# Splitting the modulation projection of a transformer layer kernel: the part needed first by feature, the rest by weight slabs inside the next projection

## The chip, the cores and the metric

The kernel runs on one core of a Trainium2 chip. A core has TensorE (PE, matrix multiplication; its weight loads are shown as PEld), VectorE (DVE), ScalarE (ACT), GpSimd (POOL) and SyncE (SP, which here only issues DMAs), and 16 DMA engines that move data between HBM and the on-chip memory SBUF. The metric is the device time of one execution in microseconds (us); the lower, the better.

## The reference, cut to what matters

One layer works on 1024 prompt rows and 32 sample rows of 1024 features. Both sub-layers take a normalised input that is scaled and shifted by a conditioning vector; prompt and sample have one vector each.

```python
def adaln(c, w_ada, b_ada):
    return jnp.split(jax.nn.silu(c) @ w_ada + b_ada, 6, axis=-1)

def modulate(x, g, shift, scale):
    return rmsnorm(x, g) * (1.0 + scale[:, None, :]) + shift[:, None, :]
...
        p_sh1, p_sc1, p_gt1, p_sh2, p_sc2, p_gt2 = adaln(c_prompt, w_ada[l], b_ada[l])
        mp, new_p = mix_prompt(modulate(yp, g_mix_pre[l], p_sh1, p_sc1), w_in[l], w_out[l], ...)
        yp = yp + p_gt1[:, None, :] * rmsnorm(mp, g_mix_post[l])
        fp = swiglu(modulate(yp, g_ffn_pre[l], p_sh2, p_sc2), w_gate[l], w_up[l], w_down[l])
        yp = yp + p_gt2[:, None, :] * rmsnorm(fp, g_ffn_post[l])
```

`w_ada` is 1024 x 6144 floats (25 MB), and its six groups of 1024 columns are shift, scale and gate of the mixing part and shift, scale and gate of the feed-forward part. Only the first two groups are needed before `mix_prompt` projects its input with `w_in`; everything is float32.

## The kernel before

The kernel is a sequence of blocks. In a block each engine has its own instruction stream, the streams meet at semaphores, and a block ends when every stream has ended. The change touches the first two blocks.

`conditioning` computes all 6144 modulation values for the two conditioning vectors. SP loads `w_ada` in 12 column blocks of 512 (2 MB each) into three buffers in turn, with the input rows `x` (four loads of 1 MB and one of the 32 sample rows) between them, and then three pieces of `w_in`. PE takes each column block as 8 matmuls with the two vectors as a 2-column weight and 512 streamed columns (line 299), DVE adds the bias (line 311). The result is a row per vector. To use shift and scale as a value per partition, POOL writes the rows to HBM and reads them back 4 bytes at a time (lines 263 and 267). Meanwhile ACT squares and sums the rows of `x` (line 283), POOL takes the power -0.5 (line 271) and DVE normalises the nine row tiles of `x` (line 329). DVE also makes two bias strips, 8 partitions (one for each head) of 768 and 384 values.

`natural` starts with two DMAs on SP's queue that write each strip 128 times to HBM (lines 414 and 415: `[[0, P], [1, STRIP_A]]`, 3 MB and 1.5 MB, all read from 8 partitions). PE transposes `x` in 17 units (`turn_pe`, lines 352 and 355), ACT and DVE read the units back with scale and shift applied (`turn_read`). PE then projects nine row tiles with 840 columns of `w_in` (line 457: per tile 8 matmuls of 512 and 8 of 328 columns), ACT and DVE copy each tile out, and PE turns the keys (line 466). SP waits for the last tile, loads three weight pieces for the next block (line 528), stores the results (lines 435 and 438) and waits for the strips. The next block, `transposed`, continues with line 604.

Of the kernel before, what the change touches and what calls it, by code (L numbers as in the profile page):

```python
# [27 lines left out]
ALU = mybir.AluOpType  # L28
# [3 lines left out]
P = 128  # L32
D = 1024
# [102 lines left out]
def build(nc, ins, outs):  # L136
    with ExitStack() as ctx:
# [54 lines left out]


STRIPS = X + 6144


def conditioning(ctx, nc, ins, outs, sem, T, T3, B, view, ident, d_ada, **_):
    w_ada = ins["w_ada"][0].rearrange("(p t) n -> p t n", t=KT)
    c_in, b_in, tab_in = sem("c_in"), sem("b_in"), sem("tab_in")
    x_in = [sem(f"x_in{i}") for i in range(5)]  # L200
    ada_in = [sem(f"ada_in{i}") for i in range(3)]
    wnat_in = ctx.wnat_in = sem("wnat_in")
    silu_done, ada_mm, ada_row = sem("silu_done"), sem("ada_mm"), sem("ada_row")
    ss_zero, ss_done, var_done, rstd_done, xn_done = (sem(n) for n in (
        "ss_zero", "ss_done", "var_done", "rstd_done", "xn_done"))
    ident_done, strip_mm, strip_done = (sem(n) for n in (
        "ident_done", "strip_mm", "strip_done"))
    ada_out, gates_out, mod_in, mod_done = sem("ada_out"), sem("gates_out"), sem("mod_in"), sem("mod_done")
    x_at = [KA + D * t for t in range(NT)]
    tab_a, strip_a, tab_b, hot_b, strip_b = (CA + 7168, STRIPS, CA + 7456, CA + 7472, STRIPS + STRIP_A)  # L210
    junk = HT + 7296

    def x_sem(t):
        return x_in[4 if t == SAMPLE else t // 2]


    order = [0, 1, 2, 3, 6, 7, 8, 9, 4, 5, 10, 11]

    with nc.Block() as block:
        @block.sync  # L220
        def _(sp):
            sp.dma_start(T3(R_C, 2, KT)[:, 0, :], ins["c_prompt"][0].rearrange("(p t) -> p t", t=KT)).then_inc(c_in, 16)
            sp.dma_start(T3(R_C, 2, KT)[:, 1, :], ins["c_sample"][0].rearrange("(p t) -> p t", t=KT)).then_inc(c_in, 16)
            xp = ins["x_prompt"][0].rearrange("(t p) d -> p t d", p=P)
            for c in range(12):
                if c >= 3:
                    sp.wait_ge(ada_mm, c - 2)
                sp.dma_start(T3(QA + 4096 * (c % 3), KT, 512), w_ada[:, :, 512 * order[c]:512 * order[c] + 512]).then_inc(ada_in[c % 3], 16)
                if c == 1:
                    sp.dma_start(T(HT, 6 * D, 2), ins["b_ada"][0].partition_broadcast(2)).then_inc(b_in, 16)  # L230
                if 2 <= c < 6:
                    i = c - 2
                    sp.dma_start(T3(x_at[2 * i], 2, D), xp[:, 2 * i:2 * i + 2, :]).then_inc(x_in[i], 16)
                if c == 6:
                    sp.dma_start(T(x_at[SAMPLE], D, DEC), ins["x_sample"][0]).then_inc(x_in[4], 16)
            w_in = ins["w_in"][0].rearrange("(t p) n -> p t n", p=P)
            wn = T3(CA, KT, NAT_W)
            for a, b, n in ((N_VA, C_VA, 512), (N_KB, C_KB, 256), (N_KI, C_KI, 72)):
                sp.dma_start(wn[:, :, a:a + n], w_in[:, :, b:b + n]).then_inc(wnat_in, 16)
            sp.wait_ge(ada_row, 12)  # L240
            for a in (2 * D, 5 * D):
                sp.dma_start(d_ada[:, a:a + D], T(X + a, D, 2)).then_inc(gates_out, 16)
            sp.wait_ge(gates_out, 32)

        @block.gpsimd
        def _(pool):
            nc.gpsimd.memset(ident, 0.0).then_inc(ident_done, 1)
            nc.gpsimd.memset(T(R_HALF, 1), -0.5).then_inc(ident_done, 1)
            pool.wait_ge(ident_done, 2)
            nc.gpsimd.affine_select(out=ident, in_=ident, compare_op=ALU.not_equal, fill=1.0, base=0,  # L250
                                    pattern=[[-1, P]], channel_multiplier=1).then_inc(ident_done, 1)
            pool.dma_start(T(tab_a, 2 * REL + 1, HEADS), ins["rel_bias_a"][0]).then_inc(tab_in, 16)
            pool.dma_start(T(tab_b, HEADS, BUCKETS), ins["t5_bias"]).then_inc(tab_in, 16)
            pool.dma_start(T(hot_b, STRIP_B, BUCKETS), ins["t5_onehot"]).then_inc(tab_in, 16)
            for i, name in enumerate(("g_mix_pre", "g_ffn_pre")):
                pool.dma_start(T(R_G + 8 * i, KT), ins[name][0].rearrange("(t p) -> p t", p=P),
                               allow_slow_non_contiguous=True).then_inc(mod_in, 16)


            for i in range(2):  # L260
                a = 3 * D * i
                pool.wait_ge(ada_row, 4 * i + 4)
                pool.dma_start(d_ada[:, a:a + 2 * D], T(X + a, 2 * D, 2)).then_inc(ada_out, 16)
                pool.wait_ge(ada_out, 16 * i + 16)
                for j in range(2):
                    for c in range(2):
                        pool.dma_start(T(R_MOD + 16 * (2 * i + j) + 8 * c, KT),
                                       d_ada[c, a + D * j:a + D * j + D].rearrange("(t p) -> p t", p=P),
                                       allow_slow_non_contiguous=True).then_inc(mod_in, 16)
            pool.wait_ge(var_done, 1)  # L270
            nc.gpsimd.tensor_tensor(T(R_RSTD, NT), T(R_RSTD, NT), view(T(R_HALF, 1), [[0, NT]]), ALU.pow).then_inc(rstd_done, 1)

        @block.scalar
        def _(act):
            act.wait_ge(c_in, 32)
            nc.scalar.activation(T3(R_SC, KT, 2), T3(R_C, 2, KT).rearrange("p c t -> p t c"), ACT.Silu).then_inc(silu_done, 1)
            act.wait_ge(ss_zero, 1)
            for t in range(NT):
                r = rows_of(t)
                act.wait_ge(x_sem(t), 16)  # L280
                if t:
                    act.wait_ge(ss_done, t)
                nc.scalar.activation(T(junk, D, r), T(x_at[t], D, r), ACT.Square,
                                     accum_out=T(R_SS + t, 1, r)).then_inc(ss_done, 1)

        @block.tensor
        def _(pe):
            pe.wait_ge(silu_done, 1)
            for c in range(12):
                if c == 3:  # L290
                    pe.wait_ge(tab_in, 48)
                    nc.tensor.matmul(B(7, STRIP_B, HEADS), T(tab_b, HEADS, BUCKETS), T(hot_b, STRIP_B, BUCKETS),
                                     start=True, stop=True).then_inc(strip_mm, 1)
                pe.wait_ge(ada_in[c % 3], 16 * (c // 3 + 1))
                if c >= 2:
                    pe.wait_ge(ada_row, c - 1)
                w = T3(QA + 4096 * (c % 3), KT, 512)
                for k in range(KT):
                    mm = nc.tensor.matmul(B(c % 2, 512, 2), T3(R_SC, KT, 2)[:, k, :], w[:, k, :],
                                          start=(k == 0), stop=(k == KT - 1))  # L300
                mm.then_inc(ada_mm, 1)

        @block.vector
        def _(dve):
            nc.vector.memset(T(R_SS, NT), 1.0).then_inc(ss_zero, 1)
            dve.wait_ge(b_in, 16)

            def ada_rows(c):
                dve.wait_ge(ada_mm, c + 1)
                at = 512 * order[c]  # L310
                nc.vector.tensor_tensor(T(X + at, 512, 2), B(c % 2, 512, 2), T(HT + at, 512, 2), ALU.add).then_inc(ada_row, 1)

            for c in range(3):
                ada_rows(c)

            dve.wait_ge(tab_in, 48)
            tab = T(tab_a, 2 * REL + 1, HEADS)
            nc.vector.tensor_scalar(T(strip_a, 511, HEADS), view(tab, [[0, 511]], 2 * REL), -1.0, None, ALU.mult).then_inc(strip_done, 1)
            nc.vector.tensor_scalar(T(strip_a + 511, 257, HEADS), view(tab, [[-1, 257]], 2 * REL), -1.0, None, ALU.mult).then_inc(strip_done, 1)
            dve.wait_ge(strip_mm, 1)  # L320
            nc.vector.tensor_scalar(T(strip_b, STRIP_B, HEADS), B(7, STRIP_B, HEADS), -1.0, None, ALU.mult).then_inc(strip_done, 1)
            for c in range(3, 10):
                ada_rows(c)
# [1230 lines left out]
```

## Time and profile before

| what | value |
|---|---|
| median of three runs | 1933.57 us (1931.02 to 1934.14) |
| span of the profiled execution | 1930.9 us, first to last instruction |
| PE busy | 1774.0 us, 92% of the span |
| PE weight loads busy | 1436.4 us, 74% |
| DVE, ACT, POOL busy | 819.3, 651.9, 139.4 us |

The span is the time from the first to the last recorded instruction of one execution; the timed runs also contain what lies around it. In the rows below, a line number is a line of the kernel before, times are us from the start of the span unless marked ns, and the bracket at the end of a timeline row is the idle time of that engine before the row and what ended it.

### The profile page before, as it was taken

How to read it: one execution, taken by the hardware profiler on the slowest of the kernel's cores; microseconds unless marked ns; L12 is line 12 of the kernel's file. 1: busy time of each engine (PE TensorE's matmuls, PEld its weight loads, DVE VectorE, ACT ScalarE, POOL GpSimd, SP SyncE). 2: the span in 40 equal slices, each digit the busy share in tenths (PEclk: the TensorE clock that was granted, in tenths of full speed). 3: DMA queues.
4: the chain of work that ended last, by engine and by line, in shares of the span. 5: the costliest groups of instructions: out<-in, count | busy, mean ns of one | idle time of the engine just before them, and what ended most of it. 6: DMA issues, size and time to landing. Idle time of an engine off the chain costs nothing. (4 is left out here: it accounts for less than half of the span.)

```text
span 1930.9 us, 24858 instructions
## 1 busy us (share of the span) xinstructions
PE 1774.0 (92%) x9641; PEld 1436.4 (74%) x9641; DVE 819.3 (42%) x1606; ACT 651.9 (34%) x1188; POOL 139.4 (7%) x273
## 2 busy tenths in 40 slices
PE   7989799999889988899999399999999998999994
PEld 1145499994357865566654299999999998999994
DVE  0120166668899985455433411111111112444446
ACT  1010145545699953233322411111111111333332
POOL 1100000005211011111101100000000000000000
PEclk9999899999899979989999699999999998999997
DMA  9944531113000030000000311111111113200005
GB/s 344 302 80 50 157 77 44 45 35 110 1 1 1 2 134 22 22 22 23 23 23 25 114 56 43 43 44 54 43 43 43 45 42 148 92 0 0 0 0 204
DMA packets 98951, 123.44 MB, mean 64 GB/s; under 512 B 11402, under 2 KB 70866, under 8 KB 98838
## 3 DMA queue, kind: packets, MB, share of 16 engines
q1 hardware_dynamic: 96892, 116.88, 19.8%
q0 software_dynamic: 1984, 5.57, 0.9%
q8 instruction: 46, 0.75, 0.2%
q14 instruction: 29, 0.24, 0.0%
HBM read 105.44 MB, written 18.96 MB: 64 GB/s over the span
## 5 line engine op out<-in xcount | busy, mean ns | idle before, releaser
L1309 PE MATMUL ps<-h_hi,gu_hi 128*128 128x352 f32 x1056 | 341.7, 324 | 8.0 <-DVE gu_lo L1345 8.0
L1309 PE MATMUL ps<-h_lo,gu_hi 128*128 128x352 f32 x1056 | 339.3, 321 | 0.0
L1309 PE MATMUL ps<-h_hi,gu_lo 128*128 128x352 f32 x1056 | 338.9, 321 | 0.0
L918 PE MATMUL ps<-arena 128*128 128x512 f32 (+5 forms) x464 | 181.3, 508 | 35.6 <-DVE small L1110 18.2
L1309 PEld LDWEIGHTS ps<-h_hi,gu_hi 128*128 128x128 f32 x1056 | 198.8, 188 | 8.1 <-DVE gu_lo L1345 8.1
L1309 PEld LDWEIGHTS ps<-h_lo,gu_hi 128*128 128x128 f32 x1056 | 199.1, 189 | 0.0
L1309 PEld LDWEIGHTS ps<-h_hi,gu_lo 128*128 128x128 f32 x1056 | 198.5, 188 | 0.0
L1398 PE MATMUL ps<-a_hi,wd_hi 128*128 128x352 f32 x528 | 174.1, 330 | 13.9 <-DVE a_lo L1421 13.9
L905 PE MATMUL ps<-arena 128*128 128x64 f32 (+2 forms) x1280 | 165.8, 267 | 7.6 <-DVE arena L976 3.2
L1398 PE MATMUL ps<-a_lo,wd_hi 128*128 128x352 f32 x528 | 171.9, 326 | 0.0
L1398 PE MATMUL ps<-a_hi,wd_lo 128*128 128x352 f32 x528 | 171.4, 325 | 0.0
L905 PEld LDWEIGHTS ps<-arena 128*128 128x128 f32 (+2 forms) x1280 | 154.3, 186 | 11.9 <-DVE arena L976 3.6
L918 PEld LDWEIGHTS ps<-arena 128*128 128x128 f32 (+1 forms) x464 | 78.2, 194 | 99.7 <-issue 66.2
L1418 DVE TENSOR_TENSOR wd_lo<-w_down_all,wd_hi 128x1024 fp32r<-128x1024 f32 x66 | 80.8, 1225 | 147.2 <-ACT wd_hi L1410 147.2
L604 PE MATMUL ps<-ht_hi,wb_hi 128*128 128x352 f32 x384 | 128.7, 335 | 12.1 <-DVE ht_lo L641 12.1
L1001 ACT ACTIVATE arena<-arena,small 128x640 f32<-128x640 f32 (+9 forms) x144 | 108.6, 754 | 66.4 <-DVE small L1110 65.9
L1410 ACT CAST wd_hi<-w_down_all 128x1024 fp32r<-128x1024 f32 x66 | 69.1, 1047 | 183.4 <-PE ps L1398 168.0
L952 PE MATMUL ps<-arena 128*128 128x512 f32 (+1 forms) x288 | 127.4, 596 | 0.4 <-ACT arena L983 0.4
L1345 DVE TENSOR_TENSOR gu_lo<-gate_raw,gu_hi 128x1024 fp32r<-128x1024 f32 x22 | 26.9, 1225 | 233.5 <-ACT gu_hi L1323 233.5
L604 PE MATMUL ps<-ht_lo,wb_hi 128*128 128x352 f32 x384 | 125.2, 326 | 0.0
L604 PE MATMUL ps<-ht_hi,wb_lo 128*128 128x352 f32 x384 | 124.8, 325 | 0.0
L976 ACT COPY arena<-ps 128x512 f32<-128x512 f32 (+3 forms) x144 | 66.7, 463 | 169.1 <-PE ps L933 169.0
(172 smaller groups left out, 2611.7 us busy)
## 6 DMA issues: line engine op xcount, KB each, us to landing
arena<-in_w_ada SPq DMA_DIRECT2D x12, 2048.0 KB, 14.0
gate_raw<-in_w_gate SPq DMA_DIRECT2D x22, 512.0 KB, 3.6
up_raw<-in_w_up SPq DMA_DIRECT2D x22, 512.0 KB, 3.7
arena<-in_w_in SPq DMA_DIRECT2D x16, 512.0 KB, 3.5
hidden<-scratch_y SPq DMA_DIRECT2D x4, 2048.0 KB, 12.2
w_down_all<-in_w_down SPq DMA_DIRECT2D x3, 2560.0 KB, 23.6
arena<-in_x_prompt SPq DMA_DIRECT2D x4, 1024.0 KB, 16.1
arena<-in_w_out SPq DMA_DIRECT2D x2, 2048.0 KB, 10.9
```

The costliest lines, as they stand in the source:

```text
L604: mm = nc.tensor.matmul(B(3 * i + c, CH), w_cut[s % 2][a][:, P * i:P * i + P], h_cut[s % 2][b][:, CH * c:CH * c + CH], start=(k == 0 and n ...
L905: mm = nc.tensor.matmul(B(7, HD, r, c0=HD * h), T(pts[t_seq[q] % 4] + P * i, r, k), value_source(t, h, b), start=(b == 0), stop=(b == bloc ...
L918: mm = nc.tensor.matmul(ps_cols(B, s_col(s) + lo, hi - lo, r), q, key_source(t, h, lo, hi), start=True, stop=True)
L952: mm = nc.tensor.matmul(B(bank, 512, r), o, T(W_OUT[c] + 512 * half, 512), start=(c == 0), stop=(c == 7))
L976: copy(view(dst, [[P, len(full)], [1, r]]), view(src, [[P, len(full)], [1, r]])).then_inc(done, 1)
L1001: nc.scalar.activation(T(pbuf[u % NBUF], w, r), T(pbuf[u % NBUF], w, r), ACT.Exp, bias=T(R_NM + u % 16, 1, r), scale=-1.0, accum_out=T(R_S ...
L1309: mm = nc.tensor.matmul(B(3 * i + c, CH), cut[i][a][:, P * k:P * k + P], h[:, NTOK * k + CH * c:NTOK * k + CH * (c + 1)], start=(k == 0 an ...
L1345: nc.vector.tensor_tensor(cut[i][1][:, :], raw[i][:, :], cut[i][0][:, :].bitcast(F32), ALU.subtract).then_inc(cut_lo[i], 1)
L1398: mm = nc.tensor.matmul(B(m, CH), w_cut[k % 2][a][:, P * m:P * m + P], a_cut[k % 2][b][:, :], start=(k == 0 and n == 0), stop=(k == FT - 1 ...
L1410: nc.scalar.copy(w_cut[k % 2][0][:, :], wd[:, D * k:D * k + D]).then_inc(cut_hi, 1)
L1418: nc.vector.tensor_tensor(w_cut[k % 2][1][:, :], wd[:, D * k:D * k + D], w_cut[k % 2][0][:, :].bitcast(F32), ALU.subtract)
```

## The change

The two blocks become one, `front`. The columns of the mixing part's shift and scale (the first 2048 of `w_ada`) are loaded in eight pieces of 256 columns, each into a buffer of its own. For them the weights are the stationary side: 128 features by 128 rows are loaded, and the two conditioning vectors stream through, so that the result has a feature per partition and no trip through HBM. The other 4096 columns are loaded in 16 slabs, each one 128-row step of 2048 columns (1 MB), into the buffers that the pieces and earlier slabs leave. PE works on two slabs after each row tile from the second on, with four matmuls per slab into partitions 0, 32, 64 and 96 of one bank. The strips are written after slab 8 has been issued. Cut to its core; the removed `conditioning` is shown above, and unchanged lines of `natural` are left out:

```diff
-            conditioning(**S)
-            natural(**S)
+            front(**S)
...
+PIECE = 256
...
+    def piece_at(c):
+        return QA + 2048 * c if c < 6 else KA + D * NT + 2048 * (c - 6)
+    def slab_at(i):
+        return QA + 2048 * (i % 6)
...
         def _(sp):
...
+            for c in range(8):
+                sp.dma_start(T3(piece_at(c), KT, PIECE), w_ada[:, :, PIECE * c:PIECE * c + PIECE]).then_inc(piece_in[c], 16)
+                if c % 2:
+                    i = c // 2
+                    sp.dma_start(T3(x_at[2 * i], 2, D), xp[:, 2 * i:2 * i + 2, :]).then_inc(x_in[i], 16)
+            sp.dma_start(T(x_at[SAMPLE], D, DEC), ins["x_sample"][0]).then_inc(x_in[4], 16)
...
+            for i in range(16):
+                if i < 6:
+                    sp.wait_ge(piece_mm, i + 1)
+                else:
+                    sp.wait_ge(rest_mm, i - 5)
+                m, t = i // KT, i % KT
+                if m == 0:
+                    sp.dma_start(T(slab_at(i), 2048), w_ada[:, t, 3 * D:5 * D]).then_inc(slab_in[i % 6], 16)
+                else:
+                    sp.dma_start(T3(slab_at(i), 2, D), w_rest[:, t, :, 2 * D:3 * D]).then_inc(slab_in[i % 6], 16)
+                if i == 8:
+                    sp.wait_ge(strip_done, 3)
+                    sp.dma_start(d_strip_a, view(T(STRIPS, 1, HEADS), [[0, P], [1, STRIP_A]])).then_inc(strip_out, 16)
+                    sp.dma_start(d_strip_b, view(T(STRIPS + STRIP_A, 1, HEADS), [[0, P], [1, STRIP_B]])).then_inc(strip_out, 16)
             sp.wait_ge(nat_mm, NT)
             for n in range(3):
                 load_wb(n, sp, ins, T3).then_inc(wb_in[n], 16)
+            sp.wait_ge(rest_row, 8)
+            for j in range(4):
+                at = row_columns(1, j)
+                sp.dma_start(d_ada[:, at:at + 512], T(ADA_ROWS + 512, 512, 2, 32 * j)).then_inc(gates_out, 16)
...
         def _(pool):
...
+            for j in range(2):
+                pool.dma_start(T(R_BCOL + 8 * j, KT), ins["b_ada"][0, D * j:D * j + D].rearrange("(t p) -> p t", p=P),
+                               allow_slow_non_contiguous=True).then_inc(cols_in, 16)
...
+            for m in range(2):
+                for j in range(4):
+                    at = row_columns(m, j)
+                    pool.dma_start(T(ADA_BIAS + 512 * m, 512, 2, 32 * j), ins["b_ada"][0, at:at + 512].partition_broadcast(2)).then_inc(brow_in, 16)
+            pool.wait_ge(rest_row, 4)
+            for j in range(4):
+                at = row_columns(0, j)
+                pool.dma_start(d_ada[:, at:at + 512], T(ADA_ROWS, 512, 2, 32 * j)).then_inc(rest_out, 16)
...
         def _(act):
...
+            act.wait_ge(mod_done, 4)
             turn_read(nc, act, 0, turned, ht_act, ht_at, 0, T, B)
...
         def _(pe):
+            for c in range(8):
+                if c == 1:
+                    pe.wait_ge(tab_in, 48)
...
+                pe.wait_ge(piece_in[c], 16)
+                w = T3(piece_at(c), KT, PIECE)
+                for f in range(2):
+                    for k in range(KT):
+                        mm = nc.tensor.matmul(B(6, 2, c0=2 * (2 * c + f)), w[:, k, P * f:P * f + P], sc[:, k, :],
+                                              start=(k == 0), stop=(k == KT - 1))
+                mm.then_inc(piece_mm, 1)
+            pe.wait_ge(xn_done, NT)
             turn_pe(nc, pe, turned, ht_act, ht_dve, lambda t, c: T(KA + D * t + c, P, rows_of(t)), T, B, ident)
...
+            def rest(i):
+                pe.wait_ge(slab_in[i % 6], 16 * (i // 6 + 2))
+                m, k = i // KT, i % KT
+                for j in range(4):
+                    mm = nc.tensor.matmul(B(4 + m, 512, 2, 32 * j), sc[:, k, :], T(slab_at(i) + 512 * j, 512),
+                                          start=(k == 0), stop=(k == KT - 1))
+                mm.then_inc(rest_mm, 1)
             for t in range(NT):
...
+                if t:
+                    rest(2 * t - 2)
+                    rest(2 * t - 1)
             pe.wait_ge(doubled, 2 * NT)
+            pe.wait_ge(rest_row, 8)
...
         def _(dve):
...
+            dve.wait_ge(piece_mm, 8)
+            dve.wait_ge(cols_in, 64)
+            for j in range(2):
+                got = view(B(6, 1, c0=16 * j), [[1, 2], [2, KT]])
+                bias = view(T(R_BCOL + 8 * j, 1), [[0, 2], [1, KT]])
+                nc.vector.tensor_tensor(T3(R_MOD + 16 * j, 2, KT), got, bias, ALU.add).then_inc(col_done, 1)
...
+                if t in (5, SAMPLE):
+                    m = 0 if t == 5 else 1
+                    dve.wait_ge(brow_in, 128)
+                    dve.wait_ge(rest_mm, KT * m + KT)
+                    for j in range(4):
+                        nc.vector.tensor_tensor(T(ADA_ROWS + 512 * m, 512, 2, 32 * j), B(4 + m, 512, 2, 32 * j),
+                                                T(ADA_BIAS + 512 * m, 512, 2, 32 * j), ALU.add).then_inc(rest_row, 1)
...
+            dve.wait_ge(mod_in, 64)
```

## Rows read from the trace of the kernel before

**Rows 1.** The page's first line: span and instruction count.
```profile
span 1930.9 us, 24858 instructions
```

**Rows 2.** Timeline of PE, first blocks: start, duration, line, tile shapes, idle before.
```profile
60.29 42.90 PE L299 MATMUL ps<-arena,small 128*2 128x512 f32 x96 [3.64 <-DMA arena<-in_w_ada]
106.05 7.18 PE L352 MATMUL ps<-small,arena 128*128 128x128 f32 x64 [2.87 <-PEq L219]
...
116.20 101.90 PE L457 MATMUL ps<-arena 128*128 128x512 f32 x288 [2.35 <-ACT arena L368]
234.98 0.66 PE L604 MATMUL ps<-ht_hi,wb_hi 128*128 128x352 f32 x1 [12.11 <-DVE ht_lo L641]
```

**Rows 3.** Timeline of SP's DMA issues; the duration is that of the issue alone.
```profile
103.93 0.55 SPq L242 DMA_DIRECT2D scratch_ada<-tail_input  x2
106.01 0.84 SPq L414 DMA_DIRECT2D scratch_strip_a<-tail_input  x1
106.91 25.38 SPq L415 DMA_DIRECT2D scratch_strip_b<-tail_input  x1
218.13 1.50 SPq L528 DMA_DIRECT2D arena<-in_w_in  x3
219.75 0.44 SPq L435 DMA_DIRECT2D out_b_k_p<-arena  x1
...
232.25 0.41 SPq L562 DMA_DIRECT2D tail_projection<-in_cache_a_k  x1
```

**Rows 4.** Busy time of engines by stretch; last three: PE clock, DMA share, GB/s.
```profile
0.00:10.00 10.00, 0.00 (x0) 0.00 (x0) 0.07 (x1) 1.50 (x2) 4.32 (x12) 1.00 0.70 201
10.00:20.00 10.00, 7.69 (x15) 1.40 (x16) 0.00 (x0) 0.00 (x0) 0.00 (x0) 1.00 1.01 344
20.00:30.00 10.00, 10.00 (x25) 1.99 (x24) 1.36 (x2) 1.90 (x3) 0.00 (x0) 1.00 1.05 394
...
140.00:160.00 20.00, 20.00 (x57) 10.65 (x56) 1.11 (x4) 0.43 (x1) 0.00 (x0) 1.00 0.47 50
...
202.00:203.00 1.00, 1.00 (x5) 0.61 (x4) 0.00 (x0) 0.00 (x0) 0.00 (x0) 1.00 0.40 48
```

**Rows 5.** DMA issues by line, 0 to 270: count, size, median us to landing.
```profile
arena<-in_x_sample SPq DMA_DIRECT2D x1, 128.0 KB, 17.9
```

**Rows 6.** Timeline of ACT, DVE and POOL around the normalising of the input.
```profile
52.17 1.06 ACT L283 ACTIVATE arena<-arena 128x1024 f32<-128x1024 f32 x1 [5.87 <-DMA arena<-in_x_prompt]
...
90.10 0.15 DVE L325 TENSOR_SCALAR small<-small 128x9 f32<-128x9 f32 x1
92.21 6.04 DVE L329 TENSOR_SCALAR arena<-arena,small 128x1024 f32<-128x1024 f32 x9 [1.96 <-POOL small L271]
98.18 0.67 DVE L311 TENSOR_TENSOR tail_input<-ps,arena 2x512 f32<-2x512 f32 x1
```

**Rows 7.** Timeline of PE: short streams behind full weight loads, mid-kernel and after idling.
```profile
603.68 1.00 PE L905 MATMUL ps<-arena 128*128 128x64 f32 x8
604.52 0.28 PE L933 MATMUL ps<-small,arena 128*128 128x128 f32 x1
...
1088.19 6.63 PE L352 MATMUL ps<-small,hidden 128*128 128x128 f32 x32 [22.00 <-ACT hidden L1255]
1099.16 6.27 PE L352 MATMUL ps<-small,hidden 128*128 128x128 f32 x32 [4.34 <-DVE hidden L1271]
```

**Rows 8.** Busy time by stretch, columns as in rows 4, in the second of those bursts.
```profile
1100.00:1105.00 5.00, 5.00 (x28) 5.00 (x27) 3.86 (x7) 4.71 (x9) 0.00 (x0) 0.55 0.00 0
```

**Rows 9.** Timeline of PE where the clock rises behind an idle stretch.
```profile
237.49 0.50 PE L604 MATMUL ps<-ht_hi,wb_lo 128*128 128x352 f32 x1
237.79 0.49 PE L604 MATMUL ps<-ht_hi,wb_hi 128*128 128x352 f32 x1
...
241.13 0.33 PE L604 MATMUL ps<-ht_hi,wb_hi 128*128 128x352 f32 x1
241.30 0.33 PE L604 MATMUL ps<-ht_lo,wb_hi 128*128 128x352 f32 x1
```

More of the change, by code:

```diff
@@ L191, in build @@
             result(hidden=hidden, **S)
[L194 to L323, printed above, removed]
-            dve.wait_ge(ss_done, NT)
-            nc.vector.tensor_scalar(T(R_RSTD, NT), T(R_SS, NT), 1.0 / D, EPS, ALU.mult, ALU.add).then_inc(var_done, 1)
-            dve.wait_ge(rstd_done, 1)
-            for t in range(NT):
-                r = rows_of(t)
-                nc.vector.tensor_scalar(T(x_at[t], D, r), T(x_at[t], D, r), T(R_RSTD + t, 1, r), None, ALU.mult).then_inc(xn_done, 1)
-            for c in range(10, 12):
-                ada_rows(c)
-            dve.wait_ge(mod_in, 160)
-            for i in range(2):
-                for c in range(2):
-                    nc.vector.scalar_tensor_tensor(T(R_SCALE + 16 * i + 8 * c, KT), T(R_MOD + 32 * i + 16 + 8 * c, KT), 1.0,
-                                                   T(R_G + 8 * i, KT), ALU.add, ALU.mult).then_inc(mod_done, 1)
@@ L391, with front @@
 HT_ACT, HT_DVE = 8 + KT, 8
-def natural(ctx, nc, ins, outs, sem, T, T3, B, view, ident, d_strip_a, d_strip_b, **_):
+STRIPS = X + 6144
+ADA_ROWS, ADA_BIAS = X + 3456, X + 4480
+R_BCOL = 840
+PIECE = 256
+def front(ctx, nc, ins, outs, sem, T, T3, B, view, ident, d_ada, d_strip_a, d_strip_b, **_):
+    w_ada = ins["w_ada"][0].rearrange("(p t) n -> p t n", t=KT)
+    w_rest = ins["w_ada"][0].rearrange("(p t) (a n) -> p t a n", t=KT, a=2)
+    c_in, cols_in, brow_in, tab_in = sem("c_in"), sem("cols_in"), sem("brow_in"), sem("tab_in")
+    x_in = [sem(f"x_in{i}") for i in range(5)]
+    slab_in = [sem(f"slab_in{i}") for i in range(6)]
+    piece_in = slab_in + [sem(f"piece_in{i}") for i in range(6, 8)]
+    wnat_in = sem("wnat_in")
+    silu_done, piece_mm, col_done, mod_done = sem("silu_done"), sem("piece_mm"), sem("col_done"), sem("mod_done")
+    rest_mm, rest_row, rest_out, gates_out, mod_in = (sem(n) for n in (
+        "rest_mm", "rest_row", "rest_out", "gates_out", "mod_in"))
+    ss_zero, ss_done, var_done, rstd_done, xn_done = (sem(n) for n in (
+        "ss_zero", "ss_done", "var_done", "rstd_done", "xn_done"))
+    ident_done, strip_mm, strip_done = (sem(n) for n in (
+        "ident_done", "strip_mm", "strip_done"))
     turned, ht_act, ht_dve = sem("turned"), sem("ht_act"), sem("ht_dve")
@@ L400, in natural, with x_sem, row_columns, k_read @@
     x_at = [KA + D * t for t in range(NT)]
+    tab_a, strip_a, tab_b, hot_b, strip_b = (CA + 7168, STRIPS, CA + 7456, CA + 7472, STRIPS + STRIP_A)
+    junk = HT + 7296
+    twice = X
     k_units = [(i, d, t0, n) for i, d in ((0, KB), (1, KB + NTOK), (2, KI))
                for t0, n in ((0, 4), (4, 4), (SAMPLE, 1))]
+    def x_sem(t):
+        return x_in[4 if t == SAMPLE else t // 2]
+    def piece_at(c):
+        return QA + 2048 * c if c < 6 else KA + D * NT + 2048 * (c - 6)
+    def slab_at(i):
+        return QA + 2048 * (i % 6)
     def ht_at(ct, lo, n):
         return T(HT + NTOK * ct + lo, n)
-    twice = X
+    def row_columns(m, j):
+        return 3 * D + 512 * j if m == 0 else (2 * D if j < 2 else 5 * D) + 512 * (j % 2)
+    def k_read(eng, odd, done):
+        for j in range(odd, len(k_units), 2):
+            col, dst, t0, n = k_units[j]
+            w = DEC if t0 == SAMPLE else P * n
+            eng.wait_ge(k_turned, j + 1)
+            copy = nc.vector.tensor_copy if odd else nc.scalar.copy
+            copy(T(dst + P * t0, w), B(2 + j % 4, w)).then_inc(done, 1)
     with nc.Block() as block:
@@ new lines, in _ @@
+        @block.scalar
+        def _(act):
+            act.wait_ge(c_in, 32)
+            nc.scalar.activation(T3(R_SC, KT, 2), T3(R_C, 2, KT).rearrange("p c t -> p t c"), ACT.Silu).then_inc(silu_done, 1)
+            act.wait_ge(ss_zero, 1)
+            for t in range(NT):
+                r = rows_of(t)
+                act.wait_ge(x_sem(t), 16)
+                if t:
+                    act.wait_ge(ss_done, t)
+                nc.scalar.activation(T(junk, D, r), T(x_at[t], D, r), ACT.Square,
+                                     accum_out=T(R_SS + t, 1, r)).then_inc(ss_done, 1)
+            act.wait_ge(mod_done, 4)
+            turn_read(nc, act, 0, turned, ht_act, ht_at, 0, T, B)
+            for t in range(NT):
+                r = rows_of(t)
+                act.wait_ge(nat_mm, t + 1)
+                nc.scalar.copy(T(NAT + NAT_W * t + 512, NAT_W - 512, r), B(1 if t % 2 else 7, NAT_W - 512, r)).then_inc(nat_act, 1)
+            k_read(act, 0, k_act)
@@ L467, in _ @@
                 mm.then_inc(k_turned, 1)
-        def k_read(eng, odd, done):
-            for j in range(odd, len(k_units), 2):
-                col, dst, t0, n = k_units[j]
-                w = DEC if t0 == SAMPLE else P * n
-                eng.wait_ge(k_turned, j + 1)
-                copy = nc.vector.tensor_copy if odd else nc.scalar.copy
-                copy(T(dst + P * t0, w), B(2 + j % 4, w)).then_inc(done, 1)
-        @block.scalar
-        def _(act):
-            turn_read(nc, act, 0, turned, ht_act, ht_at, 0, T, B)
+        @block.vector
@@ L488, in _ @@
+            dve.wait_ge(mod_done, 4)
             turn_read(nc, dve, 1, turned, ht_dve, ht_at, 0, T, B)
@@ L504, in _ @@
             k_read(dve, 1, k_dve)
+            dve.wait_ge(mod_in, 64)
+            for c in range(2):
+                nc.vector.scalar_tensor_tensor(T(R_SCALE + 16 + 8 * c, KT), T(R_MOD + 48 + 8 * c, KT), 1.0,
+                                               T(R_G + 8, KT), ALU.add, ALU.mult).then_inc(mod_done, 2)
 NCH = 3
```

61 lines of the change are left out of this document (53 added, 8 removed).

## The prediction

> **What bounds the kernel now.** I read the page first: one execution spans 1930.9 us [rows 1], and PE is busy almost throughout. So a change in the first two blocks is worth what it does to the moment at which the next block starts, 232.25 us, when SP issues the first load of `transposed` [rows 3]; the other 1698.6 us are untouched. Then I read PE's timeline [rows 2]. Four stretches follow each other: the modulation, whose last six column blocks run from 60.29 to 103.19 us; the transposes from 106.05; the nine row tiles from 116.20 to 218.10 (11.32 us each); and idling until 234.98. The last stretch is not PE's own: SP issues DMAs from 218.13 until the block ends [rows 3]. What sets the end is therefore PE's work in order, and behind it a 14.1 us tail of SP.
>
> The third view is SP's own timeline beside the DMA stretches, for the change puts new loads among these issues. The two strip writes are issued at 106.01 and 106.91 us, and the second holds SP for 25.38 us [rows 3]. Until 203 us the DMA engines then move 48 to 50 GB/s, against 394 when weights stream in, at a busy share of 0.40 to 0.47 [rows 4]. So 4.7 MB take 97 us. In the kernel before this costs nothing: it lies wholly beside the transposes and row tiles, and SP has nothing to load before 218.13.
>
> **The change, part by part.** *Modulation ahead of the transposes.* The stream before the transposes is now 8 pieces (8.39 MB), the prompt rows (4.19) and the sample rows (0.13), 12.7 MB. By 20 us some 5.45 MB can have moved, then 0.394 MB per us [rows 4]: the last rows land at about 39 us. ACT needs 1.06 us and a short read-out for each of the last three row tiles [rows 6], so the squares end at about 43. From variance to normalised rows took 90.10 to 98.25 [rows 6]; here they are ready at about 51. The pieces of `w_in` come next on the queue and land by about 48.
>
> The pieces cost PE 8 x 16 = 128 matmuls. A float32 matmul shows as two instructions (144 matmuls of the row tiles are x288 [rows 2]), so 256, each with a full 128x128 weight load and two streamed columns. No row has that form. Cheap end: eight matmuls with full loads and 64 columns take 0.84 us in the middle of dense work, 0.105 each [rows 7], 27 us in all; the pieces then end near 40, hidden by the normalising. Dear end: 32 transposes behind idle time take 6.27 and 6.63 us, 0.2 each [rows 7], at a granted clock of 0.55 (near the 1.2 GHz level) through the second burst [rows 8]: 51 us. I take the dear end, since here too PE comes from idling and does nothing but full loads with short streams. From a first landing near 8 us, the pieces end at 59, and DVE's few small operations make it 60. The transposes, 10.15 us before [rows 2], cost 16 at that clock (64 x 0.2 and 3 for the sample's reads). The row tiles start at **76 us** (62 with the cheap price: 51, 10.15 and a little) instead of 116.20: 40 us won (54).
>
> *The rest in slabs.* Each of 16 slabs is four matmuls, eight instructions, of the shape of line 299, which takes 42.90/96 = 0.447 us per instruction [rows 2]. Dear end: one after another, 3.5 us. Cheap end: all four column groups at once, 0.9. No row shows two matmuls running side by side. The two instructions of one matmul use the same columns, so in order only neighbours of different groups can overlap; I take half the serial price, **1.75 us** a slab. The line-299 row is serial and stays the dear bound. The Trainium skill has a price too ("TensorE: Matmul & The Clock Gate", Part 3, packing small matmuls): three column tiles of 512 columns ran 2.38 times as fast as one after another. By that, as an estimate, a slab is 1.5 us and the sum below comes out about 3 us lower; nothing in the rows here confirms or denies it.
>
> *The strips, moved.* They are now issued behind slab 8, which waits for slab 2's matmuls, at the end of row tile 2: 76 + 3 x 11.32 + 3 x 1.75 + 0.6 = **116 us**. Slabs 9 to 15 stand behind them on SP's queue. The copies are as before, from the same 8 partitions, so they hold for 97 us, until 213. That a transfer waits for those ahead of it on this queue is seen in the sample rows: 128 KB took 17.9 us to land behind larger loads [rows 5]; and the second strip's issue was itself held 25.38 us while the first drained [rows 3]. Slab 9 then lands at about **217** (1.05 MB at 394 GB/s and a microsecond). PE, in order, wants it behind row tile 5, at 76 + 6 x 11.32 + 9 x 1.75 = 160. It waits **57 us**, and everything of PE queues behind: row tiles 6 to 8 and the key transposes; ACT and DVE wait for those. This stall goes on to the end, for the later slabs come at once behind slab 9.
>
> *After the stall.* Slab 9 (1.75), three row tiles (34.0), slabs 10 to 13 (7.0), and 3 us because the clock has fallen: behind idle time matmuls start 0.29 us apart at first and 0.16 from about 241, 6 us after the start at 234.98 [rows 2, 9]. The last row tile ends at **263**. Then slabs 14 and 15 (3.5), DVE's four bias additions (0.68 each at line 311 [rows 6], 2.7, and 0.3 to begin), the four gate writes on SP (0.55 for two [rows 3], 1.1), and the stores, which took 219.75 to 232.25 [rows 3], 12.5. The block ends at **283.1** instead of 232.25: **51 us later**.
>
> *What costs nothing.* POOL's bias-row loads, row writes and read-backs, and DVE's additions behind tile 5 (2.7 us), lie beside row tiles; a tile's copies are not needed until two tiles on. DVE's wait for the read-backs comes at its very end, with over 90 us of room. The removed HBM trip of the mixing part's values was short and partly hidden already; what it saves is in the 76. If the stall were gone, the cover of all these would still be the 100 us of row tiles.
>
> The span of the profiled execution was 1930.9, the median of the timed runs 1933.57, which I take as 2.7 us around it. 1933.6 + 51 gives **1984 us**.
>
> **The rivals.** *Pieces at the cheap price.* The row tiles start 14 us earlier, the strips too, and all behind them: 1970. For it: 0.105 in dense work [rows 7]; against: the bursts behind idling [rows 7, 8].
>
> *Column groups that do not overlap.* A slab of 3.5 us enters the path ten times (three before the strips, seven behind slab 9), 17.5 us more: 2002 (1988 with cheap pieces). For it: the only row of this shape is serial [rows 2]. With all four at once, 8.7 less: 1975.
>
> *Slabs that pass the strips* (the other side). The mechanism is that later transfers flow on while the strips trickle. For it: under half of the DMA time is busy then [rows 4]. Against: the 17.9 and 25.38 us above. The last row tile would end at 76 + 101.9 + 14 x 1.75 = 202, the block 20 us later at 222.5: 10 us faster, **1924** (1910 with cheap pieces; with serial slabs it is slower after all, near 1950). It decides once the strips hold slab 9 for 46 us or less, against 97. The Trainium skill speaks against this rival, and so against the change ("DMA: Bandwidth & Descriptors", Queues, rings and completion order): SP has one ring on each DMA engine, consumed in order, and a DMA is complete only when all its engines are. The share of 0.47 fits a copy that keeps half the engines; by the rule the idle half helps no slab to complete. My chance stands on the rows alone.
>
> **How the numbers follow.** Strips block, pieces dear, some overlap of column groups: 0.35, 1984 (its own range 1975 to 1992). Blocked, pieces cheap, some overlap: 0.26, 1970. Blocked and serial: 0.24, 1988 to 2002. Slabs pass: 0.15, of which 0.03 with serial slabs ends slower. The range runs over the blocked cases with the bounds of both prices, the lowest being 1961 and the highest 2002: **1959 to 2004** holds 0.83. Leaving out the passing case puts 0.15 outside. A change of 0.2% is 3.9 us, about what a measurement of this kernel can tell from none; no case centres there, so same 0.02, faster 0.11, slower 0.87.
>
> **What would show it.** Right: one PE wait of 40 to 65 us on a slab's DMA between row tiles 5 and 6, DMA near 50 GB/s for 97 us from the strips' issue, row tiles that start at 62 to 76, and `transposed` starting some 35 to 65 us later than at 232.25. The piece matmuls' spacing (0.1 or 0.2 us) and the granted clock before the transposes settle the first price; the starts of a slab's eight instructions settle the second. Wrong: slabs 9 to 14 landing while the strips still run, or strips that take far less than 97 us, for instance because their speed here was set by something else than their 8 partitions.

## The result

The changed kernel takes 1978.53 us (median of 4 runs, 1972.51 to 1980.15), against 1933.68 us of the kernel before in the same session: a ratio of 1.0227, 95% interval 1.021 to 1.0244. It is slower by 45 us. The profiled span is 1975.8 us instead of 1930.9 [rows 1], also 45 us more.

### The profile page after: what moved, and what is told of

The parts are those of the page before. It is cut to its first block and busy times, and to the rows that moved or that the text cites. A ratio compares the mean times of both kernels' runs of the same rounds, so it can differ in the third digit from the quotient of the medians.

```text
span 1975.8 us, 25248 instructions
## 1 busy us (share of the span) xinstructions
PE 1768.6 (90%) x9833; PEld 1484.0 (75%) x9833; DVE 818.2 (41%) x1604; ACT 651.7 (33%) x1188; POOL 141.5 (7%) x281
## 6 DMA issues: line engine op xcount, KB each, us to landing
arena<-in_x_prompt SPq DMA_DIRECT2D x4, 1024.0 KB, 12.9
```

## The profile after

PE's timeline of the first block answers to [rows 2]. Line 433 is the pieces, 205 and 208 the transposes, 461 the row tiles, 449 the slabs and 628 the next block.

```profile
9.29 6.96 PE L433 MATMUL ps<-small,arena 128*128 128x2 f32 x32 [9.29 <-DMA arena<-in_w_ada]
...
17.55 47.95 PE L433 MATMUL ps<-small,arena 128*128 128x2 f32 x224
65.36 9.92 PE L205 MATMUL ps<-small,arena 128*128 128x128 f32 x64
...
78.24 24.30 PE L461 MATMUL ps<-arena 128*128 128x512 f32 x64 [2.35 <-ACT arena L221]
102.46 1.90 PE L449 MATMUL ps<-arena,small 128*2 128x512 f32 x16
104.29 11.55 PE L461 MATMUL ps<-arena 128*128 128x512 f32 x32
...
155.69 1.04 PE L449 MATMUL ps<-arena,small 128*2 128x512 f32 x8
219.56 1.88 PE L449 MATMUL ps<-arena,small 128*2 128x512 f32 x8 [62.83 <-DMA arena<-in_w_ada]
221.38 13.12 PE L461 MATMUL ps<-arena 128*128 128x512 f32 x32
...
279.90 0.66 PE L628 MATMUL ps<-ht_hi,wb_hi 128*128 128x352 f32 x1 [9.05 <-DVE ht_lo L665]
```

The row tiles start at 78.24 instead of 116.20. PE does slab 8 at 155.69 and then idles 62.83 us for the DMA of slab 9. DVE's timeline shows the rows normalised at 54.75, while the pieces still run:

```profile
48.71 6.04 DVE L492 TENSOR_SCALAR arena<-arena,small 128x1024 f32<-128x1024 f32 x9 [1.96 <-POOL small L384]
```

SP's timeline answers to [rows 3]. Lines 334 and 335 are the strips, 331 the slabs, 552 the next block's weights, and 586 the start of that block.

```profile
116.87 0.38 SPq L331 DMA_DIRECT2D arena<-in_w_ada  x1
117.29 0.88 SPq L334 DMA_DIRECT2D scratch_strip_a<-tail_input  x1
118.22 24.34 SPq L335 DMA_DIRECT2D scratch_strip_b<-tail_input  x1
142.60 79.27 SPq L331 DMA_DIRECT2D arena<-in_w_ada  x7
260.93 1.47 SPq L552 DMA_DIRECT2D arena<-in_w_in  x3
...
277.16 0.40 SPq L586 DMA_DIRECT2D tail_projection<-in_cache_a_k  x1
```

The stretches answer to [rows 4], with the same columns.

```profile
140.00:160.00 20.00, 16.73 (x65) 7.75 (x63) 4.71 (x10) 0.86 (x2) 0.14 (x1) 0.99 0.46 50
160.00:180.00 20.00, 0.00 (x0) 0.00 (x0) 0.00 (x0) 0.00 (x0) 1.83 (x4) 0.50 0.47 50
...
190.00:200.00 10.00, 0.00 (x0) 0.00 (x0) 0.00 (x0) 0.00 (x0) 0.00 (x0) 0.50 0.72 126
...
205.00:210.00 5.00, 0.00 (x0) 0.00 (x0) 0.00 (x0) 0.00 (x0) 0.00 (x0) 0.50 0.73 157
...
215.00:220.00 5.00, 0.44 (x4) 0.11 (x8) 0.00 (x0) 0.00 (x0) 0.00 (x0) 0.50 0.93 323
```

The strips run at 50 GB/s and share 0.47, as before. What is new is that PE has nothing to do beside them. SP's issue of slab 9 alone lasts 50.9 us, from 142.60 to 193.52. From 194 us on slabs flow beside the rest of the strips, which is why 126 and 157 GB/s stand in these stretches, 2.4 MB by 217. Yet none is complete before the last strip packet ends at 216.6: slab 9 lands at 219.5, the next five between 222.1 and 233.0.

The 45 us add up. The start of the row tiles gives -38.0. From there to the last tile's end at 260.9 it is 182.7 us instead of 101.9, so +80.8: the wait of 62.8, fourteen slabs at 0.915 (12.8), slow first work (24.30 for the first two tiles, 13.12 for the one behind the wait, 1.88 for slab 9) 4.2, and 1.0 that stays unresolved. The tail from there to the block's end is 16.3 instead of 14.1, +2.1. Together that is +44.9, and 277.16 - 232.25 is 44.9. Shifted by 45 us, the rest of the trace is as before: between 285 and 1960 us PE is busy 1567.5 us, and 1565.9 in the same stretches before.

## The experiments

Theory A: the strips, ahead of slabs 9 to 15 on SP's queue, hold them for as long as eight source partitions need. Theory B: the slabs would be late anyway, since copies and slabs share the DMA engines. Later runs ask what the strips' speed depends on, what a slab costs, and what sets the price of the pieces. Each result is a median with its range, and its ratio to the kernel before in the same session.

**The strips on another queue.** POOL issues them, at 54.5 us.

```diff
-                if i == 8:
-                    sp.wait_ge(strip_done, 3)
-                    sp.dma_start(d_strip_a, view(T(STRIPS, 1, HEADS), [[0, P], [1, STRIP_A]]))
-                    sp.dma_start(d_strip_b, view(T(STRIPS + STRIP_A, 1, HEADS), [[0, P], [1, STRIP_B]]))
...
+            pool.wait_ge(strip_done, 3)
+            pool.dma_start(d_strip_a, view(T(STRIPS, 1, HEADS), [[0, P], [1, STRIP_A]]))
+            pool.dma_start(d_strip_b, view(T(STRIPS + STRIP_A, 1, HEADS), [[0, P], [1, STRIP_B]]))
```

> The changed kernel with its two strip writes issued on POOL's queue (behind the bias rows, at about 54 us) instead of SP's behind slab 8. Theory, order on SP's queue: slab 9 no longer stands behind the strips, PE's wait of 62.8 us goes to under 3 us, the last row tile ends near 78.2 + 101.6 + 14 x 0.92 = 193 us, the next block starts near 209 instead of 277: about 1910 us. The strips themselves still take about 97 us. Rival, the strips' eight engines or source partitions block the slabs whatever the queue: every slab that lands while the strips run comes late, PE waits 20 to 60 us in all, 1930 to 1978 us.

Measured: 1920.48 us (1917.89 to 1921.82), ratio 0.9928 [0.991, 0.9945]. PE's timeline and a stretch of this run:

```profile
151.38 1.89 PE L448 MATMUL ps<-arena,small 128*2 128x512 f32 x8 [7.60 <-DMA arena<-in_w_ada]
```
```profile
105.00:115.00 10.00, 10.00 (x29) 5.20 (x28) 0.00 (x0) 0.00 (x0) 0.00 (x0) 1.00 0.94 50
```

The wait falls from 62.8 to 7.6 us, and is now for slab 7: the queue is the main cause. Sharing the engines is the likely rest. Slabs beside the strips take 28.9 us to land (median), up to 55.2, and in the stretch shown SP's queue moves no slab data, though slabs 6 and 7 were issued at 103.9 and 104.8. The strips here keep nearly all 16 engines busy, 0.94, and still move only 50 GB/s. So the number of engines did not set their speed.

**The strips by way of HBM.** Each strip goes once to HBM, and in the old place is spread from there, the 128 copies outermost.

```diff
+            sp.dma_start(d_row_a, T(STRIPS, STRIP_A, HEADS))
+            sp.dma_start(d_row_b, T(STRIPS + STRIP_A, STRIP_B, HEADS))
...
-                    sp.dma_start(d_strip_a, view(T(STRIPS, 1, HEADS), [[0, P], [1, STRIP_A]]))
+                    sp.dma_start(dst.rearrange("h p n -> p h n"),
+                                 bass.AP(row.tensor, 0, [[0, P], [n, HEADS], [1, n]]))
```

> The strips stay on SP's queue behind slab 8, but each is written to HBM once (36 KB in all) and spread to its 128 copies there, with the 128 copies as the outermost dimension. Theory, the 97 us come from the source's 8 partitions (and the 8-way split): the spread runs at 150 to 200 GB/s, 25 to 32 us, slab 9 lands near 150 before PE wants it at 157, and the time is that of the run with the strips elsewhere, about 1910 us. Rival, the 3 KB writes to HBM themselves are slow: near 50 GB/s again, PE waits some 60 us, about 1978 us.

Measured: 1909.98 us (1906.1 to 1911.27), ratio 0.9872 [0.9852, 0.9891]. SP's timeline and a stretch of this run:

```profile
117.99 1.39 SPq L340 DMA_DIRECT2D scratch_strip_a<-strip_row_a  x1
119.42 1.18 SPq L340 DMA_DIRECT2D scratch_strip_b<-strip_row_b  x1
120.64 38.07 SPq L336 DMA_DIRECT2D arena<-in_w_ada  x7
```
```profile
125.00:130.00 5.00, 5.00 (x21) 2.99 (x24) 0.12 (x1) 0.12 (x1) 0.00 (x0) 1.00 1.03 366
```

The same queue and the same bytes, but the strips land within 20 us and PE waits for no slab. The 68.6 us to the changed kernel are what the strips cost there; with them out of the way the change gains 24 us. This run changes two things, the source and the outermost dimension; the run with the heads outermost, below, keeps them apart.

**The strips behind the last slab.** Same queue, same source.

```diff
-                if i == 8:
...
+            sp.wait_ge(strip_done, 3)
+            sp.dma_start(d_strip_a, view(T(STRIPS, 1, HEADS), [[0, P], [1, STRIP_A]]))
+            sp.dma_start(d_strip_b, view(T(STRIPS + STRIP_A, 1, HEADS), [[0, P], [1, STRIP_B]]))
```

> The strips are issued on SP's queue behind the last slab (about 158 us) instead of behind slab 8. Theory, order on the queue: PE waits for no slab and its last row tile ends near 193, but the strips hold the queue for 97 us, to about 255, and the weight loads and stores behind them and the block's end wait: the next block starts at 257 to 262, 1959 to 1964 us. Rival, the strips only hurt what shares their engines at the same time: the next block starts near 209, 1910 us.

Measured: 1969.77 us (1967.17 to 1971.28), ratio 1.0187 [1.0168, 1.0206]. SP's timeline:

```profile
192.96 51.81 SPq L551 DMA_DIRECT2D arena<-in_w_in  x3
244.81 11.47 SPq L341 DMA_DIRECT2D scratch_ada<-tail_input  x4
```

PE now waits for no slab, and its tiles end at 193. But the next block's weights queue behind the strips: the issue of three takes 51.81 us instead of 1.47. The stall moves on. The result writes behind it run from 256.40 to 267.93, where the next block was expected at 257 to 262: these are the 6 us above the expectation.

**The spread from HBM, heads outermost.** As by way of HBM, but with 8 outermost, as in the original copies.

```diff
-                                 bass.AP(row.tensor, 0, [[0, P], [n, HEADS], [1, n]])
+                                 bass.AP(row.tensor, 0, [[n, HEADS], [0, P], [1, n]])
```

> The version with the strips spread in HBM, but with the 8 heads outermost in the copy instead of the 128 copies, so that it splits eight ways as the strip write of the changed kernel does, with HBM as the source. If the 8 source partitions set the 97 us: the spread stays far below that, 25 to 45 us, the DMA share near half while it runs alone, and the time is within 5 us of 1910. If the eight-way split set it: some 97 us again, PE waits about 60 us for slab 9, about 1975 us.

Measured: 1906.3 us (one run). A stretch:

```profile
125.00:130.00 5.00, 5.00 (x26) 1.85 (x25) 1.03 (x3) 0.43 (x1) 0.00 (x0) 1.00 0.51 209
```

The share is about half, as in the original copies, yet 209 GB/s pass instead of 50. So what sets 50 is the source, eight partitions of SBUF. The runs change the source and not the number of its partitions. That SBUF as such is not so slow shows in a result write of the changed kernel, 1 MB from 128 partitions, which landed 6.6 us after its issue, so at 159 GB/s or more (its list of DMA issues):

```profile
out_a_v_p<-arena SPq DMA_DIRECT2D x1, 1024.0 KB, 6.6
```

**One column group.** On the base of the kernel by way of HBM, a slab's four matmuls go to the same 32 partitions.

```diff
-                    mm = nc.tensor.matmul(B(4 + m, 512, 2, 32 * j), sc[:, k, :], T(slab_at(i) + 512 * j, 512),
-                                          start=(k == 0), stop=(k == KT - 1))
+                    mm = nc.tensor.matmul(B(4 + m, 512, 2), sc[:, k, :], T(slab_at(i) + 512 * j, 512),
+                                          start=(k == 0 and j == 0), stop=(k == KT - 1 and j == 3))
```

> The version with the strips spread in HBM (1910 us), but the four matmuls of a slab all go to the first 32 partitions of their bank (their sums are added up in one row, so the rest of the modulation is not that of the reference). Theory, the 0.915 us per slab in the changed kernel's trace is four column groups running side by side: here eight instructions at 0.43 us follow one another, 3.44 us a slab, 16 x 2.5 = 40 us more: 1950 us. Rival, the spacing of 0.43 us between every fourth instruction has another cause (waiting for weights, or a record that is missing) and groups matter little: 1910 to 1920 us.

Measured: 1947.66 us (1947.41 to 1947.79), ratio 1.0075 [1.0059, 1.0092], 37.7 us above its base. PE's timeline, two slabs:

```profile
99.57 7.03 PE L455 MATMUL ps<-arena,small 128*2 128x512 f32 x16
```

A slab takes 3.5 us in one group (7.03/2), and 0.915 in four (from 102.46 to 104.29 for two, above): 3.8 times as fast.

**Wider streams.** The pieces stream 64 columns, the two vectors 32 times over, on the base of the changed kernel.

```diff
-                        mm = nc.tensor.matmul(B(6, 2, c0=2 * (2 * c + f)), w[:, k, P * f:P * f + P], sc[:, k, :],
+                        mm = nc.tensor.matmul(B(6 if c < 4 else 0, 64, c0=64 * ((2 * c + f) % KT)), w[:, k, P * f:P * f + P],
+                                              view(T(R_SC + 2 * k, 1), [[0, 32], [1, 2]]),
```

> The changed kernel with the two conditioning vectors streamed 32 times over in each piece matmul (64 columns instead of 2; one copy is read). Theory, the pieces' 0.21 us per instruction is the lower clock and denser streams raise it: the spacing falls to about 0.105 us within the first pieces, the pieces end near 40 to 45, the transposes start when the rows are normalised (54.8 instead of 65.4), the row tiles near 66 to 70 instead of 78.2, the time falls by 8 to 12 us to 1967 to 1970. Rival, 0.21 us is the price of a full float32 load with a short stream: the spacing and the time stay (1978, within 2).

Measured: 1972.71 us (1971.11 to 1980.05), ratio 1.0209 [1.0181, 1.0238]. PE's timeline:

```profile
17.35 48.05 PE L433 MATMUL ps<-small,arena 128*128 128x64 f32 x224
```

0.214 us per instruction, as with two columns. The same shape takes 0.105 in mid-kernel [rows 7], so the form doesn't make the price. The changed kernel's own transposes, also full weight loads, show the step from one price to the other. Here are two stretches of them:

```profile
69.00:71.00 2.00, 2.00 (x12) 2.00 (x11) 1.05 (x2) 0.78 (x1) 0.00 (x0) 1.00 0.00 0
71.00:73.00 2.00, 2.00 (x20) 2.00 (x19) 1.68 (x3) 1.51 (x2) 0.00 (x0) 1.00 0.00 0
```

They start 0.214 us apart, like the pieces, and 0.109 apart from 71.0, where the trace has its first record of a granted clock, 1.00. The ranges of this kernel and the changed one overlap; no gain is shown.

**Dense work between the pieces.** Idle matmuls of 512 columns: four at the start, two ahead of each further piece, four behind the last; base by way of HBM.

```diff
+            def dense(n):
+                for _ in range(n):
+                    nc.tensor.matmul(B(1, 512), ident, view(ident, [[0, 4], [1, P]]), start=True, stop=True)
+            dense(4)
...
+                if c:
+                    dense(2)
```

> The version with the strips spread in HBM (1910 us), with idle matmuls of 512 columns put on PE (results unread): 4 while the first piece is on its way, 2 ahead of each further piece, 4 behind the last. Theory, the 0.21 us per piece instruction is the lower clock, which short streams do not lift, 64 columns neither: with the dense matmuls the spacing falls to about 0.107 us within a few pieces, all end near 50 to 55, the transposes start when the rows are normalised (about 54.8), the row tiles near 66 instead of 77.5: 1898 to 1901 us. Rival, 0.21 us is the form's own price here: the pieces still take 55 us, the dense matmuls add 15 to 25 us, the row tiles start near 95: 1925 to 1935 us.

Measured: 1926.3 us (1912.03 to 1933.2, 7 runs), ratio 0.9949 [0.9918, 0.9981]: 16 us above its base, so the expectation of 1898 to 1901 missed. PE's timeline and the stretches:

```profile
30.15 3.74 PE L448 MATMUL ps<-small,arena 128*128 128x2 f32 x32
...
51.53 6.83 PE L448 MATMUL ps<-small,arena 128*128 128x2 f32 x32
```
```profile
30.00:40.00 10.00, 10.00 (x64) 7.96 (x62) 0.00 (x0) 2.30 (x4) 0.00 (x0) 0.82 1.07 371
...
50.00:60.00 10.00, 10.00 (x37) 8.00 (x36) 5.18 (x8) 0.00 (x0) 4.63 (x7) 0.50 1.06 398
```

One piece takes 3.74 us where the mean granted clock is 0.82, and 6.83 where it is 0.50, the 1.2 GHz level: the price is the clock's. So the time falls in the rival's range, but not for the rival's cause. The dense work lifted the clock for three pieces of eight only: the pieces take 45 us instead of 55, and the dense matmuls between and behind them 32 more. The seven runs lie 21 us apart; the two shortest (1912.03 and 1915.39) have a mean granted clock of 0.944 or more over the span, the others 0.935 to 0.939.

**Less dense work, rows earlier.** One idle matmul ahead of each further piece, none behind the last, and the input rows loaded one behind each of the first four pieces.

```diff
-                    dense(2)
+                    dense(1)
...
-                if c % 2:
-                    i = c // 2
+                if c < 4:
```

> As the run with dense matmuls, but with one ahead of each further piece and none behind the last, and with the input rows loaded one 1 MB block behind each of the first four pieces, so that they are normalised near 40 instead of 54.8. Theory: PE sets the start of the transposes, at 44 to 46 if one dense matmul per piece keeps the clock up; row tiles from about 56; 1888 to 1892 us. Rival, one per piece is too few and the pieces fall back to 0.21 us each: they end near 70, row tiles near 81, 1913 us.

Measured: 1921.2 us (1919.19 to 1924.09), ratio 0.9944 [0.9927, 0.9961]. Every piece from the second on takes 6.8 to 7.0 us at a granted clock of 0.50, as in PE's timeline:

```profile
26.59 6.83 PE L448 MATMUL ps<-small,arena 128*128 128x2 f32 x32
```

So the rival's cause came, at a price above its 1913: the row tiles start at 88.12 instead of 81. The rows were normalised at 44.4 and nothing followed, since the pieces, not the rows, set the start.

**The mixing part in slabs too.** Base: heads outermost. The first 2048 columns come in eight slabs with the vectors as weight, in four column groups; ACT copies the rows and PE turns them with 16 small transposes.

```diff
-                sp.dma_start(T3(piece_at(c), KT, PIECE), w_ada[:, :, PIECE * c:PIECE * c + PIECE])
+                sp.dma_start(T(piece_at(c), 2 * D), w_ada[:, c, 0:2 * D])
...
+                for j in range(4):
+                    mm = nc.tensor.matmul(B(0, 512, 2, 32 * j), sc[:, c, :], T(piece_at(c) + 512 * j, 512),
+                                          start=(c == 0), stop=(c == KT - 1))
+                mm.then_inc(piece_mm, 1)
+            pe.wait_ge(rest_row, 4)
+            for b in range(2 * KT):
+                mm = nc.tensor.transpose(B(6, 2, c0=2 * b), T(HT + P * b, P, 2), ident[0:2, 0:2])
```

> Base: the kernel of the run by head (1906.3 us), the strips read from HBM with the heads outermost. Here the first 2048 columns too are computed as slabs: eight loads of 128 features by 2048 columns in the places of the eight pieces, four matmuls a slab in the four column groups, ACT copies the four results to a row per vector, and PE turns the row into features with 16 small transposes. If 256 instructions with a full weight load and two streamed columns at 0.214 us are what sets the start of the transposes (65.1 us), PE needs only about 8 x 0.9 to 1.8 us here, the start moves to the normalised rows at about 54.5 us, the row tiles to about 66 to 67 us, and the time comes to 1895 to 1898 us. Rival: what sets it is the arrival of the data, or PE's half clock makes the slabs dear (3.5 us each or more); then the row turning ends behind 60 us and the time stays at 1902 to 1907 us.

Measured: 1893.23 us (1891.58 to 1893.55), ratio 0.9796 [0.9779, 0.9812]. PE's timeline:

```profile
34.71 1.88 PE L439 MATMUL ps<-arena,small 128*2 128x512 f32 x8 [0.61 <-DMA arena<-in_w_ada]
43.49 1.86 PE L445 MATMUL ps<-small,arena 2*128 2x2 f32 x16 [6.90 <-ACT arena L419]
49.43 10.06 PE L205 MATMUL ps<-small,arena 128*128 128x128 f32 x64 [4.07 <-DVE arena L503]
...
62.44 24.35 PE L472 MATMUL ps<-arena 128*128 128x512 f32 x64 [2.35 <-ACT arena L221]
```

The pieces were what set the start: now the rows do (DVE, line 503). They are normalised 5 us sooner than foreseen, at 49.4, since the same 1 MB loads with longer runs (2048 columns of a row instead of 256) land sooner: 420 GB/s between 20 and 30 us, against 368 by way of HBM.

**And the rows earlier.** As above, with the row loads one behind each of the first four slabs.

```diff
-                if c % 2:
-                    i = c // 2
+                if c < 4:
```

> As the run with slabs first, and the four loads of input rows go one behind each of the first four slabs instead of one behind every second. The rows are then normalised at about 43 us instead of 54.5, the last slab lands at about 43 us, ACT's copies and the 16 small transposes end at about 49 us, the transposes start there and the row tiles at about 61 to 62 us: 1889 to 1892 us. Rival: the slabs from HBM land later because the rows go ahead of them, and the copies and small transposes follow at half clock; then the transposes start at 54 us or later and nothing is won over the run with slabs first.

Measured: 1888.46 us (1884.99 to 1892.33), ratio 0.9775 [0.9755, 0.9794], the fastest of all kernels here. PE's timeline:

```profile
42.85 1.86 PE L445 MATMUL ps<-small,arena 2*128 2x2 f32 x16 [2.48 <-ACT arena L419]
44.64 9.36 PE L205 MATMUL ps<-small,arena 128*128 128x128 f32 x64
...
56.97 22.83 PE L472 MATMUL ps<-arena 128*128 128x512 f32 x64 [2.35 <-ACT arena L221]
```

Earlier rows are worth something only now that no piece stands ahead of them: the row tiles start at 56.97 instead of 62.44. The transposes now follow the last slab and the turned rows. The ranges of the two runs overlap a little (1891.58 to 1892.33), so the 5 us rest on the two profiles, which agree with the medians.

## Why the prediction was right

The mechanism came as forecast, and the forecast of 1984 was 5 us above the median, inside its range. That it came so near is in part luck, for errors of both signs met: the pieces and slab 9 came later, the slabs and the tail were shorter. By its steps:

- *Pieces at the dear price: right.* 0.214 us per instruction against the 0.2 taken. PE starts on the pieces at 9.29, and the transposes start at 65.36 (60 foreseen). The cheap price exists, but needs the other clock level, as the transposes from 71.0 on and the run with dense work show. The row tiles start at 78.24 (76), only 2 us late, for the transposes took 12.9 us and not the 16 of the lower clock throughout. The rows were normalised at 54.75 (51), ahead of the pieces' end, so the pieces set the start; the run with the mixing part in slabs shows it.
- *A slab at 1.75 us: mis-sized.* The step failed where it said that in order only neighbours of different groups can overlap. It measured 0.915 us, the cheap bound. The timeline of PE's weight loads, changed kernel, shows a pair of slabs:

```profile
102.46 0.11 PEld L449 LDWEIGHTS ps<-arena,small 128*2 128x2 f32 x8 [0.45 <-issue]
102.89 0.10 PEld L449 LDWEIGHTS ps<-arena,small 128*2 128x2 f32 x4 [0.33 <-issue]
103.32 0.11 PEld L449 LDWEIGHTS ps<-arena,small 128*2 128x2 f32 x4 [0.32 <-issue]
```

  The 16 loads come in batches 0.43 us apart, four of them per batch behind the first, so all four column groups run side by side. The Trainium skill has 2.38 times for three column tiles ("TensorE: Matmul & The Clock Gate", Part 3, packing small matmuls); the trace points the same way with 3.8 for four. By the prediction's count ten slabs stand on the path, three ahead of the strips and seven behind slab 9's landing, so the path was overpriced by some 8 us; the six between only move time into the wait.
- *The strips hold SP's queue to 213, slab 9 at 217: right.* Issued at 117.3 (116), last packet ended at 216.6, slab 9 used at 219.56 (217). The wait is 62.8 us (57), longer because the cheap slabs brought PE there 3.3 us sooner, at 156.7 instead of 160, and because slab 9 came 2.6 us later. That is why the slab price, wrong by half, moved the end so little. The five slabs from the wait to the last tile, 9 to 13, took 5.4 us instead of 8.75.
- *After the stall: the clock cost less than taken,* 13.12 - 11.55 = 1.6 us instead of 3, beside a first slab at 1.88 instead of 0.92, together 2.5. The last row tile ends at 260.9 (263), the block at 277.16 (283.1). Of the 6 us, 2 are there by the last tile; the other 4 are the tail, 16.3 us where the prediction had 20.1. SP's gate writes begin 4.7 us behind the tile instead of 6.5, with slabs 14 and 15 done within 2 us of it, and the stores took 10.3 us instead of 12.5.
- *Why the strips are slow: right, but only assumed.* That the eight partitions set 50 GB/s was carried over from [rows 4]. The runs show that the source sets it: 50 GB/s with a share of 0.47 and of 0.94 from eight partitions of SBUF, and 209 at 0.51 from HBM. The number of partitions itself was not varied. The Trainium skill has a rule for it ("SBUF — State Buffer", Door 1, the DMA port swizzle): a transfer is limited by the SBUF ports that its partitions reach, 27.2 GB/s each, and partitions 0 to 7 reach two. By that, as an estimate, the strips could get 54 GB/s; the measured 50 agrees.

Of the rivals, cheap pieces, serial slabs and slabs that pass the strips did not come; all four groups at once did, for which the prediction had 1975. Slabs did flow beside the strips from 194 us on, but none landed before the strips ended. The passing case needed the strips to hold slab 9 for 46 us or less. By way of HBM that was met, and the kernel was faster, at 1910 against the 1924 of that rival.

What stays open: why two idle matmuls between the pieces lifted the clock for three of them and not for the others, and whether the 7.6 us with POOL's queue are the shared engines alone, which only the landing times and the stretch without slab data suggest.

## What to carry to other kernels

Before a load is put behind a bulk transfer on the same queue, work out how long that transfer drains; if it reads a few partitions, copy it once to HBM and spread it from there. When a stall moves on as its transfer is moved along the queue, change the transfer, not its place. A thin vector was better here as the stationary side, with column groups to fill the array, than as the streamed one: 256 full weight loads cost 55 us at the lower clock, eight slabs for the same columns some 2 us each, hidden by the loads.

## What was unexpected of the hardware

PE's clock stayed low through 56 us of pieces one behind the other. By way of HBM, PE and its weight loads are both busy for all of this stretch, at the same 0.21 us per instruction as the changed kernel:

```profile
20.00:30.00 10.00, 10.00 (x48) 10.00 (x48) 0.00 (x0) 2.30 (x4) 0.00 (x0) 1.00 1.08 368
```

The clock column says 1.00 here, yet 48 instructions in 10 us is about the rate of a piece at 0.50 in the runs with dense work (6.83 us for 32). The trace has no record of the granted clock before 69.7 us, where it rises to 1.00 during the transposes. Ahead of the first such record in a span, the spacing of the instructions is to be believed and not the column.
